# Scores of rotary heads over all 128 rows, from query copies with the other head's rows zero

## The reference, cut to what matters

```
# layer 0, differential: 16 score heads in 8 pairs
s = jnp.einsum('bqhd,bkhd->bhqk', qb, k).astype(jnp.float32) * scale
pr = jax.nn.softmax(s, axis=-1).reshape(B, H, 2, DIFF_Q_BLOCK, S)
a = (pr[:, :, 0] - lam_full * pr[:, :, 1]).astype(v.dtype)
return jnp.einsum('bhqk,bkhe->bqhe', a, v)
# layer 1, windowed: 16 query heads, 4 key heads
s = jnp.einsum('bnqhgd,bnchd->bnhgqc', q, kb).astype(jnp.float32) * (d ** -0.5)
```

## Time and profile before

| | us |
|---|---|
| median of 3 runs | 1103.97 |
| lowest, highest | 1102.04, 1103.98 |
| the profiled execution | 1103.54 |
| its span, first to last instruction | 1101.8 |
| busy in the span: PE, PEld | 1076.1, 956.5 |
| busy: DVE, ACT, POOL | 727.5, 584.7, 97.1 |

### The profile page before, as it was taken

The page is one execution under the profiler, slowest core; times in us unless marked ns, Lnnn a source line. Parts: engine busy times, 40 slices in busy tenths (PEclk is TensorE's granted clock), DMA queues, the critical chain, the costliest instruction groups (busy, mean ns, idle before and its releaser), DMA issues.

```text
span 1101.8 us, 17463 instructions
## 1 busy us (share of the span) xinstructions
PE 1076.1 (98%) x6920; PEld 956.5 (87%) x6920; DVE 727.5 (66%) x990; ACT 584.7 (53%) x884; POOL 97.1 (9%) x154
## 2 busy tenths in 40 slices
PE   8999999999999999999999999899999999999997
PEld 7767789999998777789999998799899989999996
DVE  6966657787777754477877766756565477555553
ACT  5656755555546646464655546534444466444442
POOL 1302000000000234200000000501000000000000
PEclk9999999999999999999999999989999999999999
DMA  8714325665543542244665554454354346655541
GB/s 297 242 64 138 115 85 184 206 214 189 192 156 140 179 138 77 77 164 156 197 222 198 162 182 166 151 180 153 116 158 149 116 150 210 195 179 200 170 138 39
DMA packets 114644, 177.51 MB, mean 161 GB/s; under 512 B 3419, under 2 KB 85524, under 8 KB 114580
## 3 DMA queue, kind: packets, MB, share of 16 engines
q1 hardware_dynamic: 114004, 175.05, 47.7%
q10 hardware_dynamic: 576, 1.57, 0.4%
HBM read 175.56 MB, written 1.05 MB: 160 GB/s over the span
## 4 chain that ended last, share of the span: by engine, by line
PE 83%; DVE 6%; ACT 4%; POOL 2%; SPq 2%; issue 1%; DMA 1%; ACTq 0%; POOLq 0%; DVEq 0%
PE ps L1794 79%; DVE wlo L1183 3%; ACT whi L674 2%; PE ps L1868 1%; PE ps L2267 1%; POOL scr L576 1%; ACT scr L809 1%; PE ps L1914 1%; POOL xn L604 1%; DMA raw<-in_diff_w_qkv 0%; PE ps L2040 0%; DMA raw<-in_swa_w_qkv 0%; DVE scr L1327 0%; SPq L437 0%; PE ps L2389 0%
## 5 line engine op out<-in xcount | busy, mean ns | idle before, releaser
L1183 DVE TENSOR_TENSOR wlo<-raw,whi 128x2048 fp32r<-128x2048 f32 x150 | 343.5, 2297 | 89.2 <-ACT whi L674 88.0
L1794 PE MATMUL ps<-xhi,whi 128*128 128x256 f32 x1248 | 356.4, 286 | 0.0
L1794 PE MATMUL ps<-xlo,whi 128*128 128x256 f32 x1248 | 354.1, 284 | 0.0
L1794 PE MATMUL ps<-xhi,wlo 128*128 128x256 f32 x1248 | 354.1, 284 | 0.0
L674 ACT ACTIVATE whi<-raw 128x2048 fp32r<-128x2048 f32 x150 | 284.7, 1909 | 60.9 <-PE ps L1794 38.5
L1794 PEld LDWEIGHTS ps<-xhi,whi 128*128 128x128 f32 x1248 | 240.5, 193 | 3.9 <-issue 1.4
L1794 PEld LDWEIGHTS ps<-xlo,whi 128*128 128x128 f32 x1248 | 240.5, 193 | 1.2
L1794 PEld LDWEIGHTS ps<-xhi,wlo 128*128 128x128 f32 x1248 | 240.4, 193 | 0.0
L1794 PE MATMUL ps<-whi,ohi 128*128 128x512 f32 x368 | 125.4, 399 | 0.0
L809 ACT ACTIVATE scr<-scr,cwT 128x256 f32<-128x256 f32 x88 | 48.1, 594 | 142.3 <-DVE scr L1327 142.3
L1794 PE MATMUL ps<-whi,olo 128*128 128x512 f32 x368 | 122.7, 392 | 0.0
(11 more groups left out here) (188 smaller groups left out, 1129.6 us busy)
## 6 DMA issues: line engine op xcount, KB each, us to landing
raw<-in_ffn_w_up SPq DMA_DIRECT2D x44, 1024.0 KB, 5.1
raw<-in_w_in SPq DMA_DIRECT2D x23, 1024.0 KB, 5.3
raw<-in_ffn_w_down SPq DMA_DIRECT2D x22, 1024.0 KB, 5.0
raw<-in_w_mlp_in SPq DMA_DIRECT2D x16, 1024.0 KB, 5.4
raw<-in_w_mlp_out SPq DMA_DIRECT2D x16, 1024.0 KB, 4.9
raw<-in_diff_w_qkv SPq DMA_DIRECT2D x11, 1024.0 KB, 5.4
raw<-in_ple_w_gate SPq DMA_DIRECT2D x8, 1024.0 KB, 4.9
raw<-in_swa_w_qkv SPq DMA_DIRECT2D x6, 1024.0 KB, 5.2
```

The lines of the kernel that those rows point to most:

```text
L1183: dve.tensor_tensor(wlo[:, u % RING, :], raw[:, u % RAW, :], whi[:, u % RING, :].bitcast(F32), ALU.subtract).then_inc(lo_ready, 1)
L1794: return pe.matmul(o, l, r, start=start, stop=stop, skip_group_check=True)
```

## The change

`qT` gets a second axis r: for each of four tiles there are two copies, copy r holding head r in its own 64 rows and zeros in the other 64. ACT writes them by two activations of 64 rows instead of one of 128. POOL zeroes the region at the start, and again after the FFN of layer 0, and a new semaphore holds the copies until then. Scores then contract over all 128 rows (the key tile holds both heads, and the other head's rows meet zeros), and in layer 0 the two heads of a block follow one another without the semaphore between them. Set B of layer 0, and tiles 4 to 7 of layer 1, now use the same four tiles of `qT` as the sets before them. The number of matmuls and their columns stay.

```
@@ -188,7 +188,7 @@
         warm = stat[:, 371:391]
 
 
-        qT = region(0, 2048, "p (a c) -> p a c", c=SEQ)
+        qT = region(0, 2048, "p (r a c) -> p r a c", r=2, c=SEQ)
         kT = region(2048, 2048, "p (a c) -> p a c", c=SEQ)
         vtm = region(4096, 2048, "p (t c) -> p t c", t=T)
         rotA = region(6144, 1024, "p (t c) -> p t c", t=T)
@@ -288,7 +288,7 @@
         v_ready = sem("v_ready")
         t_ready = sem("t_ready")
         t_free = sem("t_free")
-        head_done = sem("head_done")
+        q_zeroed = sem("q_zeroed")
         s_ready = sem("s_ready")
         max_ready = sem("max_ready")
         exp_ready = sem("exp_ready")
@@ -582,6 +582,11 @@
                     pool.tensor_tensor(ors[:, st, qt, :], ors[:, st, qt, :], nhalf[:, 0:4], ALU.pow)\
                         .then_inc(orstd_ready, 1)
 
+                def zero_other_heads():
+
+                    pool.memset(qT.rearrange("p r a c -> p (r a c)"), 0.0).then_inc(q_zeroed, 1)
+
+                zero_other_heads()
                 norm_rstd(0)
                 for c in range(2):
                     for t in range(T):
@@ -607,6 +612,8 @@
                 norm_rstd(2)
                 gate_product(0)
                 norm_rstd(3)
+                pool.wait_ge(hlo_ready[0], FT // 2)
+                zero_other_heads()
                 for c, w in ((4, 256), (5, HALF)):
                     for t in range(T):
                         rope_add(c, t, w)
@@ -899,8 +906,19 @@
                 for j in (1, 2, 3):
                     ahead(u + j)
 
-                def copy_qk(dst, tiles, t, scale):
-                    copy_T(dst[:, tiles, t * P:(t + 1) * P], ps[:, TB, :].rearrange("p (a c) -> p a c", c=P)[:, 0:tiles.stop - tiles.start, :], scale)
+                def copy_k(tiles, t):
+                    copy_T(kT[:, tiles, t * P:(t + 1) * P], ps[:, TB, :].rearrange("p (a c) -> p a c", c=P)[:, 0:tiles.stop - tiles.start, :])
+
+                def copy_q(t, zeroed):
+
+                    act.wait_ge(t_ready, tcount[0] + 1)
+                    act.wait_ge(q_zeroed, zeroed)
+                    for r in range(2):
+                        rows_ = slice(r * HD, (r + 1) * HD)
+                        ins = act.activation(qT[rows_, r, :, t * P:(t + 1) * P],
+                                             ps[rows_, TB, :].rearrange("p (a c) -> p a c", c=P), ACT.Copy, scale=0.125)
+                    ins.then_inc(t_free, 1)
+                    tcount[0] += 1
 
                 def v_copy(c, name, u, banks):
 
@@ -910,11 +928,11 @@
                             .then_inc(v_ready, 1)
 
                 for t in range(T):
-                    copy_qk(qT, slice(0, 4), t, 0.125)
+                    copy_q(t, 1)
                 ahead(u + 4)
                 ahead(u + 5)
                 for t in range(T):
-                    copy_qk(kT, slice(0, 4), t, 1.0)
+                    copy_k(slice(0, 4), t)
                 act.wait_ge(rstd_ready, 2)
                 v_copy(0, "qkv0.2", u + 5, 0)
 
@@ -938,16 +956,16 @@
                     at_copy0(s)
                     split_half()
                     if s in (5, 6):
-                        copy_qk(qT, slice(4, 8), s - 5, 0.125)
+                        copy_q(s - 5, 1)
                     if s == 7:
                         o_hi(0, 4, 0, 0, True)
                     if s:
                         o_copy0(0, s - 1)
                 o_copy0(0, N_A - 1)
                 split_half()
-                copy_qk(kT, slice(4, 8), 0, 1.0)
+                copy_k(slice(4, 8), 0)
                 split_half()
-                copy_qk(kT, slice(4, 8), 1, 1.0)
+                copy_k(slice(4, 8), 1)
                 o_hi(0, 4, 1, 1, True)
                 block_exp("B", 0, nmax[:, 8], esum[:, 8])
                 v_copy(HALF, "qkv0.5", u + 11, 2)
@@ -982,11 +1000,11 @@
                 for j in (0, 1):
                     ahead(u + j)
                 preload(5, ACT.Exp)
-                copy_qk(kT, slice(0, 2), 0, 1.0)
+                copy_k(slice(0, 2), 0)
                 ahead(u + 2)
-                copy_qk(kT, slice(0, 2), 1, 1.0)
+                copy_k(slice(0, 2), 1)
                 for t in range(T):
-                    copy_qk(qT, slice(0, 4), t, 0.125)
+                    copy_q(t, 2)
                 ahead(u + 3)
 
                 def swa_exp(s):
@@ -1012,7 +1030,7 @@
                     if s + 1 < 2 * N_A:
                         sink_exp(s + 1)
                     if s in (4, 6):
-                        copy_qk(qT, slice(4, 8), s // 2 - 2, 0.125)
+                        copy_q(s // 2 - 2, 2)
                     if s in (4, 6):
                         ple_proj(1, s // 2 - 2)
                     if s % 4 in (0, 1):
@@ -1993,24 +2011,21 @@
                 pe.wait_ge(plo_ready, 2)
                 pe.wait_ge(vecs_ready, 1)
 
-                def scores0(st, s, j):
+                def scores0(st, s):
 
 
                     qt, i = BLOCKS[s]
-                    tile = 4 * st + i
                     b = 8 * st + s
-                    if j:
-                        pe.wait_ge(head_done, b + 1)
-                    elif b > 1:
+                    if b > 1:
                         pe.wait_ge(exp_ready, b - 1)
-                    r = slice(j * HD, (j + 1) * HD)
-                    mm(ps[:, 6 + s % 2, j * SEQ:(j + 1) * SEQ], qT[r, tile, qt * P:(qt + 1) * P], kT[r, tile, :], True, True)\
-                        .then_inc(s_ready if j else head_done, 1)
+                    for j in range(2):
+                        ins = mm(ps[:, 6 + s % 2, j * SEQ:(j + 1) * SEQ], qT[:, j, i, qt * P:(qt + 1) * P], kT[:, 4 * st + i, :],
+                                 True, True)
+                    ins.then_inc(s_ready, 1)
 
                 def first_scores0(st):
-                    for j in range(2):
-                        for s in range(2):
-                            scores0(st, s, j)
+                    for s in range(2):
+                        scores0(st, s)
 
                 def probs_T0(st, s):
                     b = 8 * st + s
@@ -2063,10 +2078,8 @@
                 for s in range(N_A):
                     probs_T0(0, s)
                     if s + 2 < N_A:
-                        scores0(0, s + 2, 0)
+                        scores0(0, s + 2)
                     half(s + 1, (0,))
-                    if s + 2 < N_A:
-                        scores0(0, s + 2, 1)
                     if s in (5, 6):
                         qk_T(2, "0q1", s - 5, flat_tiles(s - 5, 4))
                     if s == 7:
@@ -2134,11 +2147,9 @@
                 for s in range(N_A):
                     probs_T0(1, s)
                     if s + 2 < N_A:
-                        scores0(1, s + 2, 0)
+                        scores0(1, s + 2)
                     if s:
                         pv0(1, s - 1)
-                    if s + 2 < N_A:
-                        scores0(1, s + 2, 1)
                     piece0(s + 1)
                 pv0(1, N_A - 1)
                 o_T0(1, 0)
@@ -2245,7 +2256,6 @@
 
                 def scores1(s):
                     g, qt, r, i = SWA_BLOCKS[s]
-                    rows_ = slice(r * HD, (r + 1) * HD)
                     if s == 0:
                         pe.wait_ge(t_free, T_USE["1q01"] + 1)
                         pe.wait_ge(rope_read, 12)
@@ -2254,7 +2264,7 @@
                     c = (1 - qt) * P
                     pair = ps[:, 6 + s % 2, :].rearrange("p (j c) -> p j c", j=2)
                     for j in range(2):
-                        mm(pair[:, j, :], qT[rows_, 4 * g + i + j, qt * P:(qt + 1) * P], kT[rows_, g, :], j == 0, False)
+                        mm(pair[:, j, :], qT[:, r, i + j, qt * P:(qt + 1) * P], kT[:, g, :], j == 0, False)
                     mm(pair[:, :, c:c + P], identb[:, :], maskb[:, qt, :].unsqueeze(1).broadcast_to([P, 2, P]), False, True)\
                         .then_inc(s_ready, 1)
```

32 lines of the change are left out of this document (15 added, 17 removed).

## The result

Nine executions of the changed kernel, in two sessions, lie between 1090.45 and 1094.04 us. The first session gave a median of 1091.83 us (4 runs) against 1103.2 us before (4 runs): a ratio of 0.9900, 95% interval 0.9889 to 0.9912. The second gave 1092.14 us (5 runs) against 1103.36. The forecast was 1091.9 us.

The account below looks back on a forecast made before the run. TensorE was taken as the bound, carrying 83% of the chain of waits. Savings of 4.65 (A) + 3.4 (B) + 4.8 (layer 1) - 0.45 - 0.25 = 12.1 us, from 1103.97, gave 1091.9 us; range 1087 to 1099.5.

Parts of the forecast that it names:

- Passes: Score matmuls on TensorE: a 128-row f32 pass over 256 columns takes 0.215 us, 0.86 us per block.
- (a): Score passes: 128-row f32 passes over 256 columns run at one cycle per column, 0.12 us; 1082.7 us, chance 8%.
- (c): Score passes: 128 rows cost twice the 64-row pass, 0.43 us, so the kernel is slower; 1118.3 us, chance 3%.
- The stall belongs to the change of row count: Weight loads around 64-row scores: idle 0.17 us before and 0.33 us after, read as the price of changing row count.
- rival (b): Part of the stall isn't the switch, or waits on ACT spread to A and layer 1; 1098.3 us, chance 12%.
- A: First head set of layer 0 (50 to 87 us): saves 4.65 us, with room on ACT and VectorE.
- B: Second head set of layer 0 (97 to 134 us): saves 3.4 instead of 5.0 us, as ACT sets the pace.
- The head start of the first two blocks is lost: Start of B: the first two blocks' saving is lost, as VectorE is still at the output transpose's split; 0.3 us.
- Layer 1: Layer 1 (398 to 467 us): sixteen blocks save 0.30 us each, 4.8 us, less 0.45 for a query copy.
- six of the eight lie beside six or more matmuls of weights: Query copies on ACT: six of eight are covered by weight matmuls; layer 1's iteration 6 is not, costing 0.45 us.
- Start: Start of layer 0: the second query transpose waits for the bank, between 0 and 0.49, taken as 0.25 us.
- Zeroing: Two memsets on POOL, at the start and behind the fourth norm, some 2 us each, hidden: cost 0.

Follow-up runs that it names:

- experiments 3 to 6: Changed kernel with 64 rows for layer 0's first head (1096.27 us), its second (1097.37), both layer 1 scores (1095.98), or layer 1's second alone (1096.53).
- experiment 10: Changed kernel with the embedding copies of B on VectorE (DVE) instead of ACT: 1091.40 us (4 runs).
- experiment 9: Changed kernel with layer 1's keys, not its queries, in two copies: 1090.74 us, ratio to before 0.9882; beside the changed kernel 1089.75 against 1092.14.

## Why the prediction was right, and where it was wrong

The time was right (1091.9 forecast, 1091.83 and 1092.14 measured), but partly by luck. By the marks the change gained 10.8 us, 1.3 less than forecast. About half of that error was met by the base it was subtracted from: the median of the three runs shown, 1103.97, lies 0.6 us above the later medians of the same kernel (1103.34 over 25 runs). And the two profiled spans differ by 12.2, close to the 12.1 forecast, only because the stretches outside the changed stages added 1.3 us net.

- **Passes**: right, 0.215 us with 128 rows; rivals (a), 0.12, and (c), 0.43, are out. The rule of the Trainium skill (TensorE: Matmul & The Clock Gate, Back-to-back issue gap) would give, by an estimate from its formula, 109 ns for 256 columns. These plain f32 passes take twice that at 64 and at 128 rows.
- **The stall belongs to the change of row count**: right (experiments 3 to 6), so rival (b) is out in its first form. Only its size is not what the idle rows say: 0.38 to 0.40 us a visit in A, 0.30 in layer 1.
- **A**: 4.65 forecast, 4.79 measured, 0.74 to 0.84 in each iteration with scores, no wait.
- **B**: 3.4 forecast, 3.68 measured, 3.40 of it in the loop, where the visits alone would give about 4.7. The forecast of a cap by ACT was right, its form was not: I made ACT the pace of every iteration. The iterations 1, 2, 3 and 5 take 2.93 to 2.98 us, nearly the 2.91 that PE would want. The loss lies in iteration 4 (3.52 us), whose exponentials stand behind ACT's embedding copies (experiment 10), and in iteration 6 (2.56 us instead of 2.05), where PV waits for ACT's output copy. Whether relieving ACT without loading DVE would give this back was not tried. "The head start of the first two blocks is lost" was wrong by 0.28.
- **Layer 1**: 4.35 forecast, 2.47 measured (78.04 - 75.57); the term that failed. The visits gave 4.06 rather than 4.8 (experiment 9 against before: 78.04 - 73.98), mostly because in iterations 5 and 6 PE meets ACT's probability copy. The second query copies took 1.59 (75.57 - 73.98) instead of 0.45; this is against a kernel that has second copies of the keys, so their full price isn't shown. The step that failed is "six of the eight lie beside six or more matmuls of weights": I looked for the PE instruction that waits for the query copy itself, and passed over what is queued behind it on ACT. The copy of iteration 4 has its cover; the probability copy, which the output transposes need and which stands behind the embedding copies, a split and two exponentials, has not. That is the second form of rival (b), at one place of one stage. The second copy was also mis-sized: it takes 0.59 to 0.60 us, as one of 128 partitions does, and with the overlap that is lost ACT's list grows by 0.72 us (1.21 against 0.48 from the query copy's start to the embedding copies), not by 0.49.
- **Start**: 0.25 forecast, 0.09 measured. **Zeroing**: hidden, as forecast; two memsets of 1.80 and 1.82 us, and the rotary addition behind the second still waits 3.61 us for its input.
- **Sum**: by the marks 10.8 us instead of 12.1. From the medians of before in the four comparisons (1103.2 to 1103.4) to that of all nine runs after (1092.1) it is 11.2.

Not tried: the two heads of a block at once in two row tiles, and 128-row scores in the third layer, where 80 loads of 64 rows are left with 3.1 us of idle time before them and no columns free in the scratch buffer for a second copy.

## What to carry to other kernels

A matmul over part of the rows among full ones pays for the change there and back, here 0.30 to 0.40 us, in layer 1 the same with two passes between as with four; padding it to full rows cost PE nothing here, since the passes kept their columns. Pad the operand that has fewer tiles and is copied off the critical stage (1.6 us more in experiment 9). When an engine beside the bottleneck gets longer work, look not only at who waits for that work but at each later entry of its list: the one with the least slack pays.

## What was not expected of the hardware

- A 64-row stretch costs the same 0.30 us with two or four passes in it (layer 1), and 0.38 to 0.40 us in loop A at either place, though the idle time in the load rows there is 0.50 and 0.69 us. Why A's visit is 0.1 us dearer than layer 1's stays open.
- ACT copies of 64x512 take as long as of 128x512, 0.59 to 0.60 us, and two in a row 1.18 to 1.20: they don't overlap as the 128x512 embedding copies behind them do, two of which take 1.09.
- Executions of one kernel differ by up to 5.0 us (1090.48 to 1095.49 in experiment 10). Half-clock stretches are shown to make up 1.4 us behind layer 0; what makes up the rest isn't shown. The marks of undisturbed stretches agree between executions to 0.01 or 0.02 us. An effect of 1 us can be read from marks and not from a few times.
